# Two buffers for the experts' bias rows, sent half a period ahead

## What is computed

```python
def expert_block(args):
    xb, e = args
    gu = xb @ w_gu[e] + b_gu[e]
    gate, up = jnp.split(gu, 2, axis=-1)
    gate = jnp.minimum(gate, SWIGLU_LIMIT)
    up = jnp.clip(up, -SWIGLU_LIMIT, SWIGLU_LIMIT)
    glu = gate * jax.nn.sigmoid(SWIGLU_ALPHA * gate)
    return ((up + 1.0) * glu) @ w_down[e] + b_down[e]
```

## Time and profile before

| | |
|---|---|
| median of 3 runs | 1581.34 us (1580.76 to 1581.83) |
| the profiled execution | 1579.49 us |
| its span | 1577.6 us |
| PE busy | 1376.6 us (87%) |
| DVE busy | 844.1 us (54%) |
| ACT busy | 727.5 us (46%) |

### The profile page before, as it was taken

How to read it: one execution, slowest core, us unless ns; L and a number is a source line. 1 busy time by engine, 2 the same in 40 slices (tenths; PEclk the granted TensorE clock), 3 DMA queues, 4 the chain that set the end, 5 groups by cost and what they waited for, 6 DMA issues and landing times.

```text
span 1577.6 us, 17803 instructions
## 1 busy us (share of the span) xinstructions
PE 1376.6 (87%) x6418; PEld 895.5 (57%) x6423; DVE 844.1 (54%) x947; ACT 727.5 (46%) x940; POOL 247.0 (16%) x318
## 2 busy tenths in 40 slices
PE   4999999999988888888797888888889788897886
PEld 1667864577663636656364674545557546566342
DVE  1567865369471726736354674453556626547134
ACT  4432354556362525744444555353555626536122
POOL 2000020212211121131111111111111112111120
PEclk9999999999988899999898999888899989998998
DMA  9655520268897979988989898897988979889796
GB/s 346 215 175 189 187 85 1 101 221 303 333 387 286 399 297 387 349 340 330 360 337 367 322 381 340 327 372 297 396 317 313 402 276 409 331 312 387 285 367 238
DMA packets 95129, 475.90 MB, mean 302 GB/s; under 512 B 23687, under 2 KB 33903, under 8 KB 42817
## 3 DMA queue, kind: packets, MB, share of 16 engines
q1 hardware_dynamic: 82656, 451.39, 73.3%
q0 software_dynamic: 12304, 23.22, 5.4%
q10 hardware_dynamic: 80, 0.13, 0.0%
HBM read 468.16 MB, written 23.09 MB: 311 GB/s over the span
## 4 chain that ended last, share of the span: by engine, by line
PE 64%; DMA 19%; ACT 7%; DVE 5%; SPq 3%; issue 2%; DVEq 0%; ACTq 0%
DMA area<-bias_g_parts 10%; PE bank L1711 9%; PE bank L1714 9%; PE bank L1744 8%; PE bank L1718 8%; DMA ring<-in_w_down 8%; PE bank L1759 4%; PE bank L1496 3%; PE bank L1308 3%; ACT e_hi L891 3%; DVE e_lo L1967 3%; PE bank L1310 3%; PE bank L1309 3%; ACT area L894 2%; SPq L590 2%
## 5 line engine op out<-in xcount | busy, mean ns | idle before, releaser
L1967 DVE TENSOR_TENSOR e_lo<-ring,e_hi 128x2048 fp32r<-128x2048 f32 x216 | 489.1, 2289 | 353.3 <-ACT e_hi L891 353.1
L891 ACT ACTIVATE e_hi<-ring 128x2048 fp32r<-128x2048 f32 x216 | 408.8, 1916 | 414.8 <-DMA ring<-in_w_down 246.1
L1711 PE MATMUL bank<-e_hi,x_hi 128*128 128x512 f32 x576 | 241.6, 419 | 0.0
L1714 PE MATMUL bank<-e_hi,x_lo 128*128 128x512 f32 x576 | 237.6, 412 | 0.0
L1744 PE MATMUL bank<-ring,area 128*64 128x512 f32 x896 | 216.8, 644 | 0.7 <-DMA ring<-in_w_gu 0.4
L1718 PE MATMUL bank<-e_lo,x_hi 128*128 128x512 f32 x576 | 161.1, 403 | 0.0
L1781 PE MATMUL bank<-e_hi,act_hi 128*128 128x512 f32 x288 | 122.7, 426 | 40.5 <-ACT e_hi L891 40.4
L1744 PEld LDWEIGHTS bank<-ring,area 128*64 128x64 f32 x896 | 66.7, 148 | 143.6 <-issue 137.9
L1711 PEld LDWEIGHTS bank<-e_hi,x_hi 128*128 128x128 f32 x576 | 116.5, 202 | 31.5 <-issue 6.6
L1714 PEld LDWEIGHTS bank<-e_hi,x_lo 128*128 128x128 f32 x576 | 116.9, 203 | 24.6
L1718 PEld LDWEIGHTS bank<-e_lo,x_hi 128*128 128x128 f32 x576 | 114.1, 198 | 25.0
(11 more groups left out here) (296 smaller groups left out, 1718.1 us busy)
## 6 DMA issues: line engine op xcount, KB each, us to landing
ring<-in_w_gu SPq DMA_DIRECT2D x256, 1024.0 KB, 7.8
ring<-in_w_down SPq DMA_DIRECT2D x128, 1024.0 KB, 8.2
ring<-in_ada_w SPq DMA_DIRECT2D x24, 1024.0 KB, 9.6
ring<-in_w_in SPq DMA_DIRECT2D x9, 1024.0 KB, 8.1
ring<-in_w_o SPq DMA_DIRECT2D x4, 1024.0 KB, 7.4
xs<-in_x SPq DMA_DIRECT2D x4, 512.0 KB, 5.2
ring<-in_w_in SPq DMA_DIRECT2D x8, 256.0 KB, 5.4
xn_rows<-area POOLq DMA_DIRECT2D x4, 512.0 KB, 4.9
```

The costliest lines, as they stand in the source:

```text
L891: return nc.scalar.activation(dst, src, ACT.Copy, scale=scale)
L1711: pe.matmul(bank[b][:], x_hi[:, c, :], hi, start=False, stop=False)
L1714: pe.matmul(bank[b][:], x_lo[:, c, :], hi, start=False, stop=False)
L1967: tt(e_lo[c % PARTS][:], raw(period.raw_slot(c)), e_hi[:, c % PARTS, :].bitcast(F32), ALU.subtract).then_inc(lo_ready, 1)
```

## The change

There are two bias buffers, `bias_pair`, and a semaphore for each, `g_rows_in0` and `g_rows_in1`; expert i uses buffer i % 2. `bias_of` and `bias_landed` pick the buffer, and the semaphore with the count that PE waits for. The bias of expert 0 is sent where it was, with that of expert 1 right behind it. In period i, SP now sends the bias of expert i + 1 between the gate/up chunks of i and the down chunks of i - 1, and waits only for the use of bias i - 1. The number of transfers, their size and PE's matmuls stay. Positions past 32, for experts with more tokens than a block holds, keep the old place and use buffer 0.

```diff
-        bias_g = view(14336, 256).bitcast(BF16)
+        bias_pair = [view(at, 256).bitcast(BF16) for at in (14336, 15952)]
...
-        g_rows_in = sem("g_rows_in")
+        g_rows_in = [sem("g_rows_in0"), sem("g_rows_in1")]
...
+        def bias_of(i):
+            return bias_pair[i % 2 if isinstance(i, int) and i < E else 0]
+
+        def bias_landed(i):
+            if isinstance(i, int) and i < E:
+                return g_rows_in[i % 2], 64 * (i // 2 + 1)
+            return g_rows_in[0], i * 64 - 64 * (E // 2 - 1)
...
             def up_bias(i, e):
 
-                if i is not 0:
+                if not isinstance(i, int) or i >= E:
                     sp.wait_ge(bias_used, i)
+                elif i > 1:
+                    sp.wait_ge(bias_used, i - 1)
+                bias_g = bias_of(i)
                 for g in range(4):
-                    sp.dma_start(bias_g[32 * g:32 * g + 3, :], bias_g_dram[g, e, :, :]).then_inc(g_rows_in, 16)
+                    sp.dma_start(bias_g[32 * g:32 * g + 3, :],
+                                 bias_g_dram[g, e, :, :]).then_inc(bias_landed(i)[0], 16)
...
                         up_bias(i, e)
+                        if i == 0:
+                            up_bias(1, 1)
...
-                    if c == 4:
+                    if c == 4 and not isinstance(i, int):
                         up_bias(i, e)
...
                     e_next = sp.value_load(expert_at[0:1, i + 1:i + 2], min_val=0, max_val=E - 1)
+                    up_bias(i + 1, e_next)
                 down_chunks(i, e_before)
...
-                pe.wait_ge(g_rows_in, i * 64 + 64)
+                pe.wait_ge(*bias_landed(i))
```

## The result

The changed kernel takes 1466.32 us (median of 4 runs, 1460.84 to 1467.54), against 1581.05 us before (4 runs): a ratio of 0.9268, 95% interval 0.9243 to 0.9292. That is 115 us less, where 101 were forecast; the time lies in the range. The profiled execution took 1465.49 us, its span is 1463.6.

A forecast was written before the change was run, and what follows sets the result against it. The loads were taken as the scarcer resource, idling because PE waits for the bias, and as the bound afterwards. 1025 + 8 + 20 + 1 = 1054 of 1152 us, a gain of 98, gave 1483, set to 1480; range 1446 to 1522.

The forecast's parts named there:

- The cause: PE's 25 bias waits, 115.7 us: the bias queues behind five 1 MB chunks, and PE's lateness idles the loads.
- (1): PE's bias waits: the bias issued 25 to 32 us ahead of need, 0 us of wait stay.
- (2): SP's own wait for the use of bias i - 1: already met before SP comes there.
- (3): SP's same four bias issues, 1.60 us, at the new place: hidden while the queue has a chunk in flight.
- (4): First period, four more issues ahead of chunk 6 of expert 0: 0 to 1.25 us, taken as 1.
- The loads without holes: Loads over a narrow and wide pair: 67.4 us by bytes at 395 GB/s, 68.3 by share, becoming the bound.
- the rival by which it would be slower: Never-resting loads share queues with gathers and scatters: if their cost doubled, 39 us more, 1520; chance 0.03.
- The kept holes: Load holes at 13 wide-to-narrow turns: 1.5 us of each kept, 20 us, as the ring's lag just fits.
- PE's side: PE over a narrow and wide pair without the bias waits: 62 to 64 us, below the loads' time.
- the one sign of the forecast that did not come: PE's waits for `ring` landings, some 60 us or more in all, at narrow chunks above all.
- (6): PE's half clock after waits: much of it goes, but 0 us in the sum as PE is no bound.
- The rate: Loads while fed: 395 GB/s, against the skill's 358 effective share and near 425 for a core streaming alone.

The follow-up runs named there:

- The run with half down chunks: The changed kernel with only the first half of each narrow expert's down chunk loaded, 29 MB less: 1450.62 us, ratio 0.9204 to the kernel before.
- ACT's other order: The changed kernel with ACT, in narrow periods, alternating splits of down chunks 2 and 3 with halves of the x rows: 1462.49 us, ratio 0.9259.

## Why the prediction came true, by its steps

**The cause.** That the bias was late because of its place behind five chunks, and that PE's lateness let the loads idle, is shown: two buffers in the old place change nothing, the early place with one buffer gives all, and both holes are gone from the trace. Sending the bias through the queue of another engine was not tried. The reading that the 6.2 us in the chain are a queue of five chunks was too much: by the packets about two were still ahead.

**(1) and (2), the waits.** No bias wait is left, as forecast, and SP's own wait costs nothing, even in the stricter form with one buffer (0.6 us).

**(3) and (4), the moved issues.** SP's four issues take 1.96 us at 555.42 and are hidden: the loads have a share of 1.00 over the pair around it. The four additional ones at the start, for which I took 1 us, are hidden too as far as the next chunk goes: it is issued at 337.95 us, against 337.79 before. The first down chunks go out 3 us later than before (386.01 against 383.08), after a stretch (325 to 350 us) in which the granted clock was 0.80 and not 1.00; whether the four have a part in that was not tried.

**The loads without holes.** 67.4 to 68.3 us a pair was forecast, 67.84 came. The rate while never resting is 394 GB/s in a pair that holds its gather and scatter; the rival by which it would be slower has fallen. That 67.84 is no proof of this step, though: the pair is held at that time by PE's side as well, as told below.

**The kept holes.** The sum kept 1.5 us at each of 13 turns, 20 us, for a ring with nothing to spare. None is to be seen: the share at the turn is 1.03. That term was mis-sized, and it is about the size of what the forecast fell short by, 98 against 114 us in the profiled execution. The reasoning behind it, that the ring would leave 12 us and need 9 to 12, was not checked by a run.

**PE's side.** This step was wrong, though it did no harm to the sum. I gave PE 62 to 64 us a pair and so left 4 us to spare, and called the loads the bound. The run with half down chunks shows that PE's side needs 68: not PE's work alone lies on it, but also the time that a freed slot's chunk stands in the queue, 13.2 us, and ACT's splits behind it. That this way round and the loads alone come to nearly the same time, 68 and 67.4 us, is luck: with a longer way round the same sum would have been too low. It fits that the waits for chunks came to 43 us and not to 60 or more, the one sign of the forecast that did not come.

**(6) The clock.** I put it at 0 as PE was to be no bound. It rose to 0.99 (0.95 or more was expected); by itself, in the kernel before, it was worth 23 us. As PE's side is at the limit in the changed kernel, it was probably a part of the gain that my sum had under another name; no run takes the clock out of the changed kernel. The argument that the lower level shows after idle times of 3 to 6 us is not quite borne out: in the kernel before it stood from 519 to 522 us too (0.50), after a wait of 2.64 us for ACT, while another of 2.62 us left the clock at 1.00 (595 to 598 us).

**The rate.** The traces' 394 GB/s in a pair, and 404 with ACT's other order, lie above 358 and below 425: for this lone core 358 is no ceiling, and the higher figure was not reached.

## What to carry to other kernels

A tiny transfer that opens a stage waits for what is still ahead of it in its queue, here some 2.75 us for each chunk of 1 MB and up to 14.5 us in all; place it by that time, not by its size. What a wait costs is not told by its length: 64.6 us of waits ahead of the wide experts gave 74 us, 51.1 ahead of the narrow ones 28. And a load share of 0.98 does not prove that loads are the bound: take the same bytes away at two different places and see which of them counts.

## What the runs showed of the hardware

GpSimd's copy of one 128x1 column, which sits ahead of each scatter, took 0.18 us each time before (183 to 195 ns over 31), and none of these 31 fell into one of DVE's splits. In the changed kernel it has a median of 2.0 us and a longest of 8.6. DVE and POOL in order of time:

```profile
594.13 1.28 DVE L2320 SCALAR_TENSOR_TENSOR area<-bank,future,area 128x1024 f32<-128x1024 f32 x1
595.33 8.89 DVE L1984 TENSOR_TENSOR e_lo<-ring,e_hi 128x2048 fp32r<-128x2048 f32 x4
595.67 8.59 POOL L837 COPY future<-routes 128x1 int32 x1 [19.17 <-DVE area L2320]
```

DVE's four splits, each with two inputs from SBUF, run back to back, and the copy that began 0.3 us into them ends with them. Of the 31 copies, twelve begin inside such a row of four and take 8.6 us each, four begin inside a row of two and take 2.0, ending about when the first of the two does, and the 15 that meet no split take 0.18 or 0.19. In the turn of a narrow expert, some 41 us earlier in the same kernel, the copy meets another kind of DVE instruction:

```profile
554.08 1.27 DVE L2000 TENSOR_TENSOR act_lo<-bank,act_hi 128x512 fp32r<-128x512 f32 x2
554.41 0.18 POOL L837 COPY future<-routes 128x1 int32 x1 [8.50 <-DVE area L2301]
```

There DVE's inputs are one from PSUM and one from SBUF, and the copy takes its 0.18 us. The Trainium skill (GPSIMD Engine Reference, Specifications) has the rule: GpSimd's way to SBUF is shared with VectorE, with contention when a DVE instruction has two SBUF inputs or is in a 2-port perf mode; the rows agree with the first of these, and add that a row of such instructions can hold a copy for all of their 8.6 us. The profile's times on POOL are rough, but the split into 0.18, 2.0 and 8.6 us is far beyond that. No wait of PE for a scatter shows, so it cost nothing that can be seen here; an experiment that keeps the two apart was not run.
